# Sixty-four bytes of offset for every weight slot and every activation row

## What is computed

```python
def swiglu(x, w_gate, w_up, w_down):            # D_FF = 2816
    return (jax.nn.silu(x @ w_gate) * (x @ w_up)) @ w_down

for l in range(DEPTH):                          # second block, DEPTH = 2
    x = x + 0.5 * swiglu(rmsnorm(x, ffn1_norm[l]), ffn1_w_gate[l], ffn1_w_up[l], ffn1_w_down[l])
    h = rmsnorm(x, mix_norm[l])
    x = x + hybrid_mixer(h, w_in[l], ...)       # projections, causal pooling, gated recurrence
    x = x + 0.5 * swiglu(rmsnorm(x, ffn2_norm[l]), ffn2_w_gate[l], ffn2_w_up[l], ffn2_w_down[l])
return rmsnorm(x, final_norm)
```

## The kernel before

| operand | before | after |
|---|---|---|
| `RAW`, `WL`, slot s | 128 in every slot | 128 + 64 s |
| `WH`, slot s | 128 in every slot | 448 + 64 s |
| `RH`, `R2H`, row k | 64 in every row | 576 + 64 k |
| `RL`, `R2L`, row k | 64 in every row | 64 + 64 k |
| `HHI`, `HLO`, each row of 256 tokens | 320 | 832 |
| `XN`, each row of 256 tokens | 128 | 768 |

## Time and profile before

### The profile page before, as it was taken

One profiled execution on the slowest core, in us unless ns is written; L12 is line 12 of the kernel. 1 busy time (PEld: TensorE's weight loads), 2 busy tenths in 40 slices (PEclk: granted clock), 3 DMA queues, 4 the chain that ended last, 5 costly groups with the idle time before them and its releaser, 6 DMA issues.

```text
span 1349.3 us, 25072 instructions
## 1 busy us (share of the span) xinstructions
PE 1317.6 (98%) x11070; PEld 1211.8 (90%) x11070; DVE 855.0 (63%) x987; ACT 700.3 (52%) x908; POOL 59.2 (4%) x70
## 2 busy tenths in 40 slices
PE   6987999999999999999999999999999999999998
PEld 5877889889999999998999998999989999899997
DVE  6998675766555577677655447555566858655553
ACT  5995566664444563365544445444465355544443
POOL 1003000000000004000000000000000500000000
PEclk9999999999999999999999999999999999999999
DMA  9216556355566475455555565556656536555552
GB/s 271 65 35 219 185 179 206 126 175 173 199 195 198 173 234 168 153 188 178 182 188 188 189 217 173 193 198 200 195 197 202 173 132 202 192 188 188 187 188 94
DMA packets 180303, 242.41 MB, mean 180 GB/s; under 512 B 7546, under 2 KB 144004, under 8 KB 180196
## 3 DMA queue, kind: packets, MB, share of 16 engines
q1 hardware_dynamic: 178260, 234.92, 53.1%
q0 software_dynamic: 1648, 5.67, 1.5%
q10 hardware_dynamic: 288, 0.22, 0.1%
HBM read 239.74 MB, written 1.05 MB: 178 GB/s over the span
## 4 chain that ended last, share of the span: by engine, by line
PE 90%; DVE 8%; issue 1%; DMA 1%; ACT 0%; DVEq 0%; ACTq 0%; POOLq 0%
PE P L414 88%; PE P L449 1%; DVE QQ L1755 1%; DMA G<-in_norm_g 1%; DVE WB L1745 0%; DVE QQ L1759 0%; DVE TMPC L1715 0%; DVE TMPC L1712 0%; DVE QQ L1746 0%; DVE X L1728 0%; DVE TMPD L1713 0%; DVE TMPD L1681 0%; DVE DB L1960 0%; PE P L704 0%; DVE GQ L1957 0%
## 5 line engine op out<-in xcount | busy, mean ns | idle before, releaser
L1448 DVE TENSOR_TENSOR WL<-RAW,WH 128x2048 fp32r<-128x2048 f32 x214 | 485.8, 2277 | 306.4 <-ACT WH L1024 305.4
L414 PE MATMUL P<-RH,WH 128*128 128x256 f32 x1856 | 516.5, 278 | 1.4 <-DVE WL L1448 1.2
L414 PE MATMUL P<-RL,WH 128*128 128x256 f32 x1856 | 513.4, 277 | 0.0
L414 PE MATMUL P<-RH,WL 128*128 128x256 f32 x1856 | 513.4, 277 | 0.0
L1024 ACT ACTIVATE WH<-RAW 128x2048 fp32r<-128x2048 f32 x214 | 406.5, 1903 | 195.4 <-DMA RAW<-in_ffn_w_down 84.7
L414 PEld LDWEIGHTS P<-RH,WH 128*128 128x128 f32 x1856 | 348.6, 188 | 3.9 <-issue 1.4
L414 PEld LDWEIGHTS P<-RL,WH 128*128 128x128 f32 x1856 | 348.6, 188 | 1.5
L414 PEld LDWEIGHTS P<-RH,WL 128*128 128x128 f32 x1856 | 348.9, 188 | 0.0
L414 PE MATMUL P<-WH,HLO 128*128 128x512 f32 x352 | 138.7, 394 | 0.0
L414 PE MATMUL P<-WL,HHI 128*128 128x512 f32 x352 | 138.0, 392 | 0.0
L414 PE MATMUL P<-WH,HHI 128*128 128x512 f32 x352 | 137.0, 389 | 0.0
(11 more groups left out here) (304 smaller groups left out, 1327.0 us busy)
## 6 DMA issues: line engine op xcount, KB each, us to landing
RAW<-in_ffn_w_gate SPq DMA_DIRECT2D x88, 512.0 KB, 4.2
RAW<-in_ffn_w_up SPq DMA_DIRECT2D x88, 512.0 KB, 5.3
RAW<-in_ffn_w_down SPq DMA_DIRECT2D x44, 1024.0 KB, 5.0
RAW<-in_w_in SPq DMA_DIRECT2D x36, 1024.0 KB, 5.1
RAW<-in_attn_w_in SPq DMA_DIRECT2D x16, 1024.0 KB, 5.4
RAW<-in_ssm_w_in SPq DMA_DIRECT2D x8, 1024.0 KB, 9.4
RAW<-in_w_out SPq DMA_DIRECT2D x8, 1024.0 KB, 5.2
RAW<-in_ssm_w_glu SPq DMA_DIRECT2D x4, 1024.0 KB, 7.4
```

Source lines behind the costliest of these rows:

```text
L414: return nc.tensor.matmul(*a, **k)
L1448: V.tensor_tensor(WL[:, s, 0:width], RAW[:, s, 0:width], WH[:, s, 0:width].bitcast(f32), SUB).then_inc(sem["lo_split"], 1)
```

## The change

Slots of `RAW`, `WL` and `WH` become 64 bytes (`STEP = 16` floats) longer, and so do the rows of `RH`, `RL`, `R2H` and `R2L`; the code goes on using the first 2048 floats of a slot and the first 256 of a row. Tensors that share the memory of `RAW`, `WL` or `WH` are pushed along to match (`STEP01`, `WH2`, `STEP3`). The memory for it comes from the fill tensors, and from `PRW`, `SPW`, `LDT` and `MS`, which now lie in memory that others use at another time. Two rows that were one run of 512 floats are now two runs of 256. The instructions of every engine and their order and waits stay the same.

```diff
@@ -19,6 +19,8 @@
 LAYERS = 2
 EPS = 1e-6
 NW = 5
+STEP = 16
+SLOT = 2048 + STEP
 LEVELS = [0, 1, 2, 4, 8, 16, 32, 64]
 LEVEL_BLOCKS = [[(0, 0), (32, 32), (64, 64), (96, 96)]] * 6 + [[(0, 32), (64, 96)], [(0, 64)]]
 POOL_WINDOWS = (2, 4, 8, 16)
@@ -113,31 +115,33 @@
 
 
         c = ExitStack()
-        RAW = sb("RAW", [128, NW, 2048], c=c)
+        RAW = sb("RAW", [128, NW, SLOT], c=c)[:, :, 0:2048]
         c.close()
         c = ExitStack()
-        sb("RAW01", [128, 2, 2048], c=c)
+        sb("RAW01", [128, 2, SLOT], c=c)
         TMPC = sb("TMPC", [128, 2048], c=c)
         UBA = sb("UBA", [128, 2, 2, JB, NCH], c=c)
         c.close()
-        WL = sb("WL", [128, NW, 2048], f32r)
+        WL = sb("WL", [128, NW, SLOT], f32r)[:, :, 0:2048]
         c = ExitStack()
         d = ExitStack()
         BRE = sb("BRE", [128, NJ, 128], c=d)
         d.close()
         TZ = sb("TZ", [128, NJ, 128], c=c)
+        sb("STEP01", [128, 2 * STEP], c=c)
         d = ExitStack()
         BIM = sb("BIM", [128, NJ, 128], c=d)
         d.close()
         KTS = sb("KTS", [128, KT, CL * 32], c=c)
-        sb("WH2", [128, 1024], c=c)
+        sb("WH2", [128, 1024 + STEP], c=c)
         UBB = sb("UBB", [128, 2, 2, JB, NCH], c=c)
+        sb("STEP3", [128, STEP], c=c)
         d = ExitStack()
         YS = sb("YS", [128, 2, DM], c=d)
         d.close()
         X4 = sb("X4", [128, NJ, NCH], c=c)
         c.close()
-        WH = sb("WH", [128, NW, 2048], f32r)
+        WH = sb("WH", [128, NW, SLOT], f32r)[:, :, 0:2048]
         c = ExitStack()
         TMPD = sb("TMPD", [128, 2048], c=c)
         c.close()
@@ -164,7 +168,7 @@
         CROW, EYE = CE[:, C_CHUNK:C_CHUNK + NCH], CE[:, C_EYE:C_EYE + 32]
 
 
-        sb("FILL0", [128, 40])
+        sb("FILL0", [128, 8])
         outer = ExitStack()
         c = ExitStack()
         PU0 = sb("PU0", [128, HH, PAD + T], c=c)
@@ -181,6 +185,11 @@
         c.close()
         BT = sb("BT", [128, 2, NJ, 128], c=big)
         CP = sb("CP", [128, 2, NJ, CL, 32], c=big)
+        c = ExitStack()
+        PRW = sb("PRW", [NROWS, 128], c=c)
+        SPW = sb("SPW", [96, 128], c=c)
+        LDT = sb("LDT", [96, 2], c=c)
+        c.close()
         TAB = sb("TAB", [128, 2, NJ, NCH], c=big)
         c = ExitStack()
         YG = sb("YG", [128, KT, T], c=c)
@@ -190,16 +199,12 @@
         SP = sb("SP", [128, 22, NJ], c=big)
         PW = sb("PW", [128, 2, CL, NJ], c=big)
         FN = sb("FN", [128, 2, CL, NJ], c=big)
-        PRW = sb("PRW", [NROWS, 128], c=big)
-        SPW = sb("SPW", [96, 128], c=big)
-        LDT = sb("LDT", [96, 2], c=big)
         big.close()
 
-        RH = sb("RH", [128, KT, T], f32r, c=outer)
-        RL = sb("RL", [128, KT, T], f32r, c=outer)
-        R2H = sb("R2H", [128, KT, T], f32r, c=outer)
-        R2L = sb("R2L", [128, KT, T], f32r, c=outer)
-        MS = sb("MS", [128, 2 * T], c=outer)
+        RH = sb("RH", [128, KT, T + STEP], f32r, c=outer)[:, :, 0:T]
+        RL = sb("RL", [128, KT, T + STEP], f32r, c=outer)[:, :, 0:T]
+        R2H = sb("R2H", [128, KT, T + STEP], f32r, c=outer)[:, :, 0:T]
+        R2L = sb("R2L", [128, KT, T + STEP], f32r, c=outer)[:, :, 0:T]
         c = ExitStack()
         CA = sb("CA", [128, C_ATTN], c=c)
         RT = sb("RT", [128, 2, 2, 2, 32], c=c)
@@ -222,7 +227,7 @@
         c.close()
         CM = sb("CM", [128, C_MIX], c=outer)
         ATB = sb("ATB", [128, 2, HH, 32], c=outer)
-        sb("FILL2", [128, 576], c=outer)
+        sb("FILL2", [128, 64], c=outer)
         c = ExitStack()
         SG = sb("SG", [128, 2, T], c=c)
         HF = sb("HF", [128, 2, T], c=c)
@@ -238,6 +243,7 @@
         ATX = sb("ATX", [128, HH, 128], c=c)
         DB = sb("DB", [128, 1024], c=c)
         OG = sb("OG", [128, 2, 512], c=c)
+        MS = sb("MS", [128, 2 * T], c=c)
         HS = sb("HS", [128, 2, 3, HH], c=c)
         GA = sb("GA", [128, 2, KT, T], c=c)
         PU = [PU0, sb("PU1", [128, HH, PAD + T], c=c), sb("PU2", [128, HH, PAD + T], c=c)]
```

## The result

| | before | after |
|---|---|---|
| median (lowest to highest) of 4 runs | 1350.57 us (1349.29 to 1353.24) | 1377.83 us (1377.38 to 1380.84) |
| span of the profiled execution | 1349.3 us | 1375.6 us |

The ratio is 1.0201, with a 95% interval of 1.0188 to 1.0215. What follows answers to the earlier trace rows: clock and span, the page's first part, the waits of TensorE, and groups by form.

What follows compares the result with a forecast made beforehand. TensorE, busy 98% of the span, was taken as the bound, through its matmul pace. 1349.3 us + 0 for all parts + 1.7 us outside the span gave 1351.0 us, range 1327 to 1372 us.

Steps and rivals of the forecast that it cites:

- the first part of the change: TensorE's streaming operand against the next weight block loaded meanwhile: new distances cost 0, between +35.9 and -42.8 us.
- six distances: Stream-to-block distances seen in the kernel before, of sixteen possible, all odd: claimed to show no difference in pace.
- the even distances: Even numbers of 64-byte steps between TensorE's operands, half of those the change brings: no row shows their pace.
- the floor: All TensorE matmuls lose every collision, 256 columns at 109 ns and 512 at 220.5 ns: -42.8 us.
- The argument from sliding: During one weight load TensorE's operands slide by 512 bytes, so a 64-byte shift changes when they meet: cost 0.
- Rival 1: Slower: TensorE's fast pace needs every row to begin alike; all matmuls slow 1387 us, half 1369 us; chance 0.27.
- ceiling: Every TensorE matmul takes the slow pace, 4.5 ns more for 256 columns and 4.9 for 512: +35.9 us.
- Rival 2: Faster: TensorE's matmul pace includes collisions, half of the distances free of them; 1330 us, all 1308 us; chance 0.25.
- Rival 3: Offsets leave pace alone, but slow TensorE stretches are drawn anew: 1349.7 to 1353.6 us; chance 0.48 with no effect.
- The second and third parts: Other engines' writes colliding with TensorE's reads, cost 0; splits writing two runs of 256, cost 0, bounded at 0.1 us.

Runs made afterwards that it cites:

- bench1: Replaces the network by short blocks of the three matmuls at sixteen starts 64 bytes apart, no other engine working: 113.3 to 120.0 ns per 256-column matmul.
- even: Kernel before, with RH, RL, R2H and R2L moved by 64 bytes as a whole, nothing staggered: 1386.40 us, ratio 1.0247.
- hhi384: Kernel before, with HHI and HLO (and what shares their memory) moved from 320 to 384 in their KB: 1364.30 us, ratio 1.0088.
- slots_aligned: Kernel with only the weight slots staggered by 64 bytes, WH pushed by 192 bytes to match WL modulo 256: 1378.15 us, ratio 1.0204.
- bench2: Short matmul blocks without the network, starts 32 bytes apart, plus 64 combinations of RH, RL and WL offsets: two combinations give 113.3 ns in both repeats.
- slots_only: Changed kernel with plain rows in RH, RL, R2H and R2L, only the weight slots staggered by 64 bytes: 1378.00 us, ratio 1.0179.
- rows_only: Changed kernel with all weight slots alike at 128, only the rows of RH, RL, R2H and R2L staggered: 1378.09 us, ratio 1.0184.
- rows256: Slots alike, rows of RH and RL staggered by 256 bytes, R2H and R2L plain, against the kernel before: 1351.37 us, ratio 0.9995.

## Why the prediction was wrong

**The step that failed** is the first part of the change, where the relation of TensorE's two readers was costed at 0 as "the value nearest to the rows". It rested on six distances without a difference. They were 1 and 9 steps for 256 columns and 3, 7, 11 and 15 for 512. Modulo four steps, 1 and 9 are the same, and 3, 7, 11 and 15 are the same: with the period of 256 bytes that bench1 shows, six samples were one sample for each kind, and both in class 3, the quickest for 256 columns and the second for 512. The prediction named the even distances as its weak point; the weak point was the period. The term measured +27.0 us where the sum had 0.

**Two readings** of rows in it were off. The 45 steps of the earlier trace rows do not pass through distances 1 and 9, nor over a step of 512 bytes. In the kernel's code (`gate_up_columns`) a stretch first takes the two column blocks that begin at 128 of their KB through both of its units, 48 matmuls, and then the two at 640; these 45 steps are all of distance 9. The even pace that the prediction claimed is there all the same. The 48 matmuls just before are of distance 1, and 39 steps within them also take 113.3 ns:

```profile
325.13 0.28 PE L414 MATMUL P<-RH,WH 128*128 128x256 f32 x1
...
329.55 0.28 PE L414 MATMUL P<-RH,WH 128*128 128x256 f32 x1
```

The 220.5 ns for plain fp32 count the last matmul to its end; from start to start they are 217.7 ns, so that the floor should have been 48.7 us in place of 42.8. It was not reached.

**The argument from sliding** (a start 64 bytes later changes when the readers meet rather than how often) falls with even: same lengths, one start moved, 113.9 to 119.9 ns. Its observation that the same offsets run at two paces was right, but "not (alone) a property of the addresses" was used as if it were not one at all. Both hold. The class decides which paces occur: no block of one class, unit or piece of class 0 or 2 ran at 113.3 ns. What TensorE ran before decides which of them is found (hhi384 and slots_aligned; 19 blocks of 24 of class 3 in bench1).

**Why the change lost all of it.** After the change, RH less WH and RL less WH are 128 + 64 (k - s) bytes, and RH less WL is -64 + 64 (k - s), all modulo 256, so each three matmuls mix two classes, and four rows k go through all four, whatever the slot. In bench2's numbers the four rows are (0,0,3), (1,1,3), (2,2,3) and (3,3,3); an estimate from its paces is (117.8 + 115.6 + 119.3 + 117.8) / 4 = 117.6 ns. Measured are 117.8, with no whole unit outside 117.6 to 118.0 (without steps over 150 ns). slots_only has the same four by slot, through the 320 bytes between WH and WL. rows_only keeps one distance in the three matmuls and goes through the classes by k; the mean of the four classes in bench1 is (120.0 + 117.8 + 118.7 + 113.3) / 4 = 117.5 ns, measured 118.0. So each half loses all. That a mixed stretch takes the mean of its parts is an estimate and not shown.

**Rival 1** had the sign and nearly the price of 256 columns (4.5 ns foretold, 3.9 measured), but its mechanism, a row that must begin where the last ended, is refuted by rows256 and by even. Its ceiling of 1387 us was too high, two thirds of it by the 512-column term: 2 to 2.5 ns each instead of 4.9, as the new distances mix classes of 226.7 to 233.3 ns. even reached 1386, with the 256-column matmuls at 119.9 ns in the mean.

**Rival 2** did not occur in the change, and no class went below 113.3 ns for 256 columns. For 512 columns a little of it exists: 226.7 ns in class 0, where the trace before had 229. **Rival 3** cannot be seen in the change, where the pieces of the earlier trace rows take 43.56 and 43.64 us, both slow. It is seen in rows256, at its own size: 42.52 us where there were 43.85. In hhi384, too, matmuls at unchanged addresses fall into the slow step, and there it costs 15.2 us, over ten times that size.

**The second and third parts were right.** VectorE and ScalarE take what they took, the wait for a split is again 1.2 us, and bench1 shows every pace without another engine. With this the sentence of the Trainium skill that the prediction cited ("SBUF — State Buffer", "Who interferes with whom") agrees as far as other engines go. The same section of the Trainium skill gives PE two independent read ports, one for the stream and one for the weight load; the runs here differ, 113.3 against 120.0 ns by the distance between these two operands alone, and the measurement decides.

**Still open:** what has the period of 256 bytes; which operand's distance counts where the three matmuls differ (bench2); why the stretch behind a down projection at 227 ns falls into the slow step; and whether a layout exists in which all 256-column stretches find 113.3 and all 512-column ones 227 ns. By the table above that would save at most some 5,929 x 0.7 + 2,075 x 2.5 ns, 9 us; the one attempt, hhi384, lost 12. No version faster than before was found.

## What to carry to other kernels

When TensorE streams one tensor and loads the next block meanwhile, in fp32r as here, choose the distance of their starts modulo 256 bytes on purpose, keep it the same in all passes and all slots, and pad in multiples of 256 bytes; here the distance is worth 2 to 2.5% of the kernel. When an effect of addresses is judged from places in a trace that seem varied, reduce them by every power of two first, since a tuned layout may have sampled one class only. A gain in one stretch has to be measured with the stretch behind it, which may pay for it.

## What the runs showed of the hardware

- In fp32r with a weight load for every matmul, the pace depends on the distance between the starts of stream and weight block, with a period of 256 bytes: 113.3, 117.8, 118.7 or 120.0 ns for 256 columns, 226.6 to 233.6 ns for 512 (bench1).
- The best class differs with the width: class 0 is the worst for 256 columns (120.0 ns) and the best for 512 (226.6 to 228.2 ns, bench1).
- The same 256-column matmuls at the same distance have two stable paces, 113.3 and 117.8 ns, in class 3 often and in class 1 now and then, and what TensorE ran before decides which one they keep: 32 of 32 stretches behind a down at 113.3 ns before, none of 32 in hhi384.
